# Zeroing the causal triangles of one attention branch on another engine, in a hybrid attention and MLP layer

## What is computed

```python
# selected branch: 16 blocks of 64 keys per query; per head
s = einsum(q, k_selected) * scale - slope * dist
p = masked_softmax(s, dist >= 0)          # causal
o_sel = einsum(p, v_selected)
# forgetting branch, per head
s = einsum(q, k) * scale + cq[..., None] - csum[:, :, None, :]
p = masked_softmax(s, tk <= tq)           # causal
o_fox = einsum(p, v)
# then
out = gates[0] * o_cmp + gates[1] * o_sel + gates[2] * o_win
y = g_a * (o_n @ w_branch_nsa) + g_b * (o_f @ w_branch_fox)
h = h + y @ w_out
h = h + square(relu(rms_norm(h) @ w_up)) @ w_down
```

## Time and profile before

| | |
|---|---|
| median of 3 runs | 1173.84 us (1173.33 to 1174.19) |
| profiled execution | 1172.47 us, of which the slowest core's span is 1171.0 us |
| spans of the 8 cores | 1168.5 to 1171.0 us |
| PE, DVE, ACT, POOL busy | 96%, 56%, 52%, 6% of the span |

### The profile page before, as it was taken

The page is one execution under the profiler, slowest core; times in us unless marked ns, Lnnn a source line. Parts: engine busy times, 40 slices in busy tenths (PEclk is TensorE's granted clock), DMA queues, the critical chain, the costliest instruction groups (busy, mean ns, idle before and its releaser), DMA issues.

```text
span 1171.0 us, 25218 instructions; the slowest of 8 cores (1168.5 to 1171.0 us)
## 1 busy us (share of the span) xinstructions
PE 1121.3 (96%) x8607; PEld 604.9 (52%) x8607; DVE 652.6 (56%) x1482; ACT 610.3 (52%) x1248; POOL 73.0 (6%) x136
## 2 busy tenths in 40 slices
PE   2998989999999999999999999999999999999997
PEld 1555665676575757644444444444444444444443
DVE  1665767655645455633434477455656474747477
ACT  4755888999999999932222355321121202030354
POOL 1000222122110000000000000000000000000000
PEclk9998999999999999999999999999999999999999
DMA  9972000002010024172041175511121111111034
GB/s 196 216 152 51 5 10 9 6 8 44 9 30 14 3 46 78 43 254 53 1 72 37 33 121 103 105 36 37 37 37 37 36 37 36 37 37 37 1 126 162
DMA packets 36122, 70.03 MB, mean 60 GB/s; under 512 B 21312, under 2 KB 22080, under 8 KB 32032
## 3 DMA queue, kind: packets, MB, share of 16 engines
q0 software_dynamic: 5184, 34.15, 16.7%
q1 hardware_dynamic: 30816, 34.28, 10.3%
HBM read 89.38 MB, written 8.39 MB: 83 GB/s over the span
## 4 chain that ended last, share of the span: by engine, by line
PE 91%; issue 3%; DVE 2%; DMA 2%; ACT 2%; DVEq 0%; SPq 0%; POOL 0%; ACTq 0%; POOLq 0%
PE bank L328 91%; DVE RG L328 2%; DMA RG<-x 2%; ACT RG L328 2%; SPq L150 0%; POOL RG L328 0%; DVEq L167 0%; DVE arena L328 0%; DVEq L160 0%; DVE uT L328 0%; ACTq L167 0%; POOLq L167 0%
## 5 line engine op out<-in xcount | busy, mean ns | idle before, releaser
L328 ACT ACTIVATE RG<-bank 128x512 bf16<-128x512 f32 (+3 forms) x888 | 452.2, 620 | 337.3 <-PE bank L328 330.9
L328 PE MATMUL bank<-uT,arena 128*128 128x512 bf16 x2048 | 490.4, 379 | 1.3 <-DVE arena L328 0.9
L328 PE MATMUL bank<-RG 128*128 128x65 bf16 (+8 forms) x3780 | 325.2, 225 | 14.0 <-DVE RG L328 11.2
L328 PEld LDWEIGHTS bank<-uT,arena 128*128 128x128 bf16 x2048 | 199.9, 98 | 214.7 <-issue 2.5
L328 DVE TENSOR_TENSOR RG<-RG,bank 128x512 f32<-128x512 f32 x320 | 218.8, 686 | 141.1 <-PE bank L328 137.8
L328 PE MATMUL bank<-arena,RG 128*128 128x512 bf16 x1280 | 277.6, 379 | 0.0
L328 PEld LDWEIGHTS bank<-RG 128*128 128x128 bf16 (+3 forms) x3780 | 199.5, 98 | 107.1 <-issue 21.9
L328 PEld LDWEIGHTS bank<-arena,RG 128*128 128x128 bf16 x1280 | 125.3, 98 | 151.0
L328 DVE TENSOR_TENSOR RG<-RG 128x512 bf16<-128x512 f32 (+3 forms) x199 | 118.0, 594 | 151.3 <-ACT RG L328 147.3
L328 ACT ACTIVATE RG<-RG 128x512 f32<-128x512 f32 (+3 forms) x149 | 86.9, 586 | 74.2 <-DVE RG L328 46.4
L328 ACT ACTIVATE RG<-bank,prm_s 128x512 f32<-128x512 f32 x64 | 43.9, 687 | 117.5 <-PE bank L328 114.8
(11 more groups left out here) (39 smaller groups left out, 273.5 us busy)
## 6 DMA issues: line engine op xcount, KB each, us to landing
arena<-wall POOLq DMA_DIRECT2D x30, 1024.0 KB, 9.7
RG<-x SPq DMA_DIRECT2D x32, 512.0 KB, 15.9
out<-RG SPq DMA_DIRECT2D x32, 256.0 KB, 2.3
RG<-c_qx SPq DMA_DIRECT2D x8, 144.0 KB
arena<-wall POOLq DMA_DIRECT2D x4, 256.0 KB, 18.1
RG<-wall POOLq DMA_DIRECT2D x1, 1024.0 KB, 12.3
arena<-wall POOLq DMA_DIRECT2D x1, 576.0 KB, 11.0
RG<-c_kx SPq DMA_DIRECT2D x4, 144.0 KB
```

Of the source, the lines that this page charges most:

```text
L328: return P.emit(eng, lambda e, method=method, kw=kw: getattr(e, method)(**kw), ins, outs, inc)
```

## The change

`diag_cut` gets an argument. For the selected units it gives one POOL instruction, `affine_select`, which keeps the elements whose query index is at least the key's partition index and fills 0.0 in the others; it reads no constant. For the forgetting units it gives the minimum on DVE as before. 96 cuts (8 heads, 4 query groups, 3 diagonal tiles) leave DVE's queue and stand in POOL's: 64 of one block and 32 of two blocks.

```diff
-        def diag_cut(pt, at_):
+        def diag_cut(pt, at_, how):
             n, st = len(at_), at_[-1] - at_[0] or 1
             blk = pt.rearrange('p (a b) -> p a b', b=128)[:, at_[0]:at_[-1] + 1:st, :]
-            E('dve', 'tensor_tensor', out=blk, in0=blk, in1=capb.unsqueeze(1).to_broadcast([128, n, 128]), op=ALU.min)
-
-        def unit_tiles(tl, kaug, qaug, K, tg, v_fn, nv, post, ob, cut=False):
+            if how == 'pool':
+                E('pool', 'affine_select', out=blk, in_=blk, pattern=[[0, n], [1, 128]], compare_op=ALU.is_ge, fill=0.0, base=0, channel_multiplier=-1)
+            else:
+                E('dve', 'tensor_tensor', out=blk, in0=blk, in1=capb.unsqueeze(1).to_broadcast([128, n, 128]), op=ALU.min)
+
+        def unit_tiles(tl, kaug, qaug, K, tg, v_fn, nv, post, ob, cut=''):
...
-                        diag_cut(PT[pt_], [c[0] // 128 for c in cuts])
+                        diag_cut(PT[pt_], [c[0] // 128 for c in cuts], cut)
...
-                                nsa_post(1, g * 4 + hl, g, hl, tg), o_bank(len(tiles), len(cl), nb[0]), True)
+                                nsa_post(1, g * 4 + hl, g, hl, tg), o_bank(len(tiles), len(cl), nb[0]), 'pool')
...
-                                        fox_post(h, tg), o_bank(len(tiles), len(cl), 2), True)
+                                        fox_post(h, tg), o_bank(len(tiles), len(cl), 2), 'dve')
```

## The result

The changed kernel takes 1180.75 us (median of 5 runs, 1179.79 us the fastest) against 1173.84 us: ratio 1.0059, 95% interval 1.0047 to 1.0070. That is 6.9 us slower where 2.7 us had been forecast. It is slower, the side that had the largest chance, and it lies in the range of 1172.3 to 1180.8, but only just, and outside the forecast's own range of 1174.8 to 1178.5.

The account below looks back on a forecast made before the run. PE, busy 96% of the span, was taken as the bound. Three early delays (0.98, 0.98, 0.97), -0.5, -0.25 and +0.5 sum to +2.7 us on 1173.84: 1176.5 us, own range 1174.8 to 1178.5, full range 1172.3 to 1180.8.

Parts of the forecast that it names:

- that of 180 to 201 us: DVE's chain there loses six cuts, one locked, so the add of 200.54 starts about 1.2 us earlier; net -0.25 us.
- rival C: Selects on POOL are dear, at the upper bounds of 0.45 and 0.73 us: about 1180.5 us; chance 0.13.
- Price of a select: On POOL, a one-block select takes 0.29 us and a two-block one 0.41: 32 us more POOL work.
- The select comes later than the cut by the length of the add: At tg = 1 units the select queues behind POOL's add; PE starts 1.11 us after the add's start, up to 0.98 later.
- ... pass in full to the end: Delays of PE up to 200 us are not made up later but reach the kernel's end in full.
- B: Rival: no difference, as PE and ACT make up part of the early units' 2.9 us; about 1174.8 us; chance 0.33.
- has no cause left: In sel(0, 3, 0) the select is done by 188.8 us, so PE's wait of 1.04 us before 190.32 goes.
- A: Rival: faster, as DVE's relief brings posts and adds earlier and covers the add before a select; about 1171.3 us; chance 0.16.
- -0.5 at 134 to 137 us: At sel(0, 0, 0) DVE's chain to a post loses three cuts, PE's own delay fits its wait: net -0.5 us.
- +0.5 for later units: Small delays of 0.1 to 0.2 us in later units, half taken up by PE or ACT: +0.5 us.
- No DVE instruction of 0.7 us where one took 0.3: Sign that the lock between DVE's cuts and POOL's adds is gone; one locked cut took 0.75 us, mean 0.318.
- From 300 us on nothing changes: Sign of a right forecast: the kernel from 300 us on is unaffected by the change.

Follow-up runs that it names:

- run 1: The changed kernel with the 24 cuts of the eight tg = 1 units back on DVE, 72 selects staying on POOL: 1174.54 us against 1174.29, ratio 1.0005.
- run 3: The changed kernel with POOL's adds written 4 steps later, behind the unit's selects, and four buffers instead of two: 1168.68 us, ratio 0.9952.
- run 4: The kernel before, all cuts on DVE, with only POOL's adds 4 steps later and four buffers: 1176.19 us against 1174.04, ratio 1.0016.
- run 5: The changed kernel with POOL's adds written one step later, between a unit's first and second select: 1175.01 us against 1173.99, ratio 1.0006.
- run 2: The kernel before with only the 24 cuts of the tg = 1 units as selects on POOL, the other 72 on DVE: 1186.23 us, ratio 1.0101.
- run 7: The changed kernel with 20 idle MATMULs before the first cut PV at the three long waits only: 1178.14 us, ratio 1.0036; changed kernel beside it 1181.26.

## Why the prediction came out as it did

The mechanism was right: a select is late by the add ahead of it, PE stands still by that much at the early units, and runs 1, 3, 4 and 5 show it. The size was not: 2.7 us forecast, 6.9 measured. What the sum lacked is the clock, and one of its terms, that of 180 to 201 us, was wrong. That 1180.75 still lies in the range is luck: its upper edge, 1180.8, was set by rival C, whose cause did not occur.

- **Price of a select:** right. 0.293 and 0.409 us against 0.29 and 0.41. C is refuted, though its time, 1180.5 us, is close to what was measured: a time alone proves no cause. By the 1.03 cycles an element that the Trainium skill (GPSIMD Engine Reference, "Performance versus the Vector engine") states for such a body, the estimate for two blocks was 0.40 us; the trace agrees, with 0.409. The factor of about two against VectorE, which the Trainium skill gives there for a two-input `tensor_tensor`, doesn't show in this select: 0.293 and 0.409 us against cuts with a median of 0.216 and 0.285 us.
- **"The select comes later than the cut by the length of the add":** right. PE starts 1.06 us behind the add's start at sel(0, 0, 1), where 1.11 was worked out, and added waits of 0.92, 0.83, 0.40, 0.94 and 0.23 us answer to 0.98, 0.98, 0.50, 0.98 and 0.15. At sel(0, 2, 1) it was 0.57 us for 0.97. There, in the kernel before, DVE stands idle for 0.46 us in the middle of the post (in front of the RECIPROCAL at 162.93 us), in the changed kernel for 0.10 us, so that the add comes earlier. Run 1 has the same gain, with a wait of 1.14 us instead of 1.49. Why that pause is gone isn't known. Runs 3 and 5 show the queue to be the cause.
- **"... pass in full to the end":** right, nearly. The stretches grow by what the waits grow by: 0.8 for 0.92 us from tile 30 to 46, 0.8 for 0.83 us from tile 62, 0.6 for 0.57 from tile 94, 0.7 for 0.94 from tile 158. B is refuted.
- **The wait in sel(0, 3, 0) that "has no cause left":** right for the wait (1.04 to 0 us). But 0.22 and 0.39 us of new waits for DVE come just behind it, so that only some 0.4 us of it are saved.
- **"So the add of 200.54 starts that much earlier", by 1.2 us, and the stretch comes to -0.25 us:** this term failed. Counted from tile 126's ACTIVATE, the add starts at 23.15 us before and at 23.08 us changed, 0.07 us earlier, and PE's first PV behind it 0.85 us later. From tile 126 to tile 186 the time grew from 34.4 to 35.1 us. I had taken DVE's 16.6 us busy of 19.9 us for one chain, but it breaks where DVE has to wait for PE. On core 0 of the changed kernel DVE, relieved of the three cuts of sel(0, 3, 1), stands idle for 1.07 us, in front of a product that has no idle time before it in the kernel before:

```profile
187.37 0.16 DVE L328 TENSOR_TENSOR RG<-bank,RG 128x4 f32<-128x4 f32 x1 [1.07 <-PE bank L328]
```

  There DVE went by PE's pace, and PE had itself stood still for 0.40 us at sel(0, 3, 1). Behind the cuts of sel(0, 3, 0) DVE copies a bank that PE has filled (COPY 32x512); it starts 15.34 us behind tile 126's ACTIVATE before and 15.32 us changed, and from it on to the add no cut stands in DVE's queue in either kernel. Before, on core 7, from PE's last MATMUL ahead of the wait to DVE's product:

```profile
197.50 0.27 PE L328 MATMUL bank<-trib,identb 128*128 128x256 bf16 x1
...
198.51 0.42 DVE L328 TENSOR_TENSOR RG<-bank,RG 128x256 f32<-128x256 f32 x1 [0.17 <-DVE RG L328]
```

and changed, on core 0:

```profile
199.12 0.27 PE L328 MATMUL bank<-trib,identb 128*128 128x256 bf16 x1
...
200.16 0.43 DVE L328 TENSOR_TENSOR RG<-bank,RG 128x256 f32<-128x256 f32 x1 [0.17 <-DVE RG L328]
...
200.73 0.67 POOL L328 TENSOR_TENSOR RG<-RG 128x256 bf16<-128x256 bf16 x1 [2.84 <-DVE RG L328]
...
201.79 0.54 PE L328 MATMUL bank<-RG 128*128 128x65 bf16 x5 [2.39 <-POOL RG L328]
```

  1.01 and 1.04 us: the six cuts fewer changed nothing there. A is refuted for the same reason; DVE's room is worth the 1.3 to 2.0 us of runs 1 and 2, not the whole.
- **The other small terms:** -0.5 at 134 to 137 us was -0.4 (tiles 46 to 62: 9.0 to 8.6 us), +0.5 for later units was +0.2. So the sum of 2.7 us on the cores at full clock is met by errors that cancel: +0.7 for -0.25 at 180 to 201 us on one side, sel(0, 2, 1) and the smaller terms on the other. That is luck too.
- **"No DVE instruction of 0.7 us where one took 0.3":** right. Before, ten of the 96 cuts took 0.48 to 0.75 us; in the changed kernel no DVE instruction of this stage stands out in this way.
- **Busy times:** POOL +27.9 us (forecast 30 to 35), DVE -21.7 us (forecast 25 to 28). Both lie outside what was given. The groups give 31.8 us and 27.7 us as worked out; but busy time counts overlapping rows once, and these instructions overlap their neighbours: by (31.8 - 27.9) / 96 = 0.04 us each on POOL and 0.06 us on DVE.
- **"From 300 us on nothing changes":** right up to tile 464 (from tile 300, at 269 us, 86.25 us before and changed).
- **The term that was missing:** the clock, 1.7 us for each stretch at 1.2 GHz, up to two on a core, about 3 us of the slowest core (run 7). I had read the granted clock of 1.00 in the earlier trace rows as a given, while the waits at three places were about to grow by 0.6 to 0.9 us. With it, 2.7 + 3.4 = 6.1 us, where 6.9 were measured. The rest, 0.8 us, isn't explained; the start of the first tile alone differs by up to 3 us between the cores of one execution (102.9 to 105.6 us before, 103.2 to 105.6 us changed).

## What to carry to other kernels

Before moving an instruction to an idle engine, look at what stands ahead of it in that engine's queue and waits for something else: here the add cost PE 0.67 us at a place and the select only some 0.1 us more than the cut that it replaced. Change the order of the two together with the move: here the same selects cost 0.6% behind an add and gain 0.5% in front of it, while the adds moved alone gain nothing. Where PE's waits grow to about 2 us, read the granted clock of every core and not only of the slowest.

## What was not expected of the hardware

In an engine that is busy for over 90% of its time, one wait of 1.76 to 2.4 us was followed by 3.4 us at 1.2 GHz on some cores and not on others, in the same execution and with the same wait: one to five of eight cores behind each of three waits in the changed kernel, seven of eight behind 2.38 us in run 2. Behind waits of up to 1.5 us none was seen from 110 to 230 us, in any run. 1.2 us of MATMULs without use inside the wait kept all cores at 2.4 GHz. What decides it for a core is open.
